# Expert products with weights standing and tokens moving, in blocks of 120 slots

## What is computed

```python
def hier_moe(xn, w_grp, b_grp, w_router, b_router, w_gate, w_up, w_down):
    ...
    eid = grp[:, None].astype(jnp.int32) * EXPERTS_PER_GROUP + top_i.astype(jnp.int32)
    ...
    def expert_block(args):
        xblk, e = args
        hid = jax.nn.silu(xblk @ w_gate[e]) * (xblk @ w_up[e])
        return hid @ w_down[e]
    ...
    return jnp.zeros_like(xn).at[tok_buf].add(yb * w_buf[:, None].astype(yb.dtype))
```

## Time and profile before

| | |
|---|---|
| median of 3 runs | 1314.06 us |
| the profiled execution | 1314.39 us, span 1312.7 us |
| granted TensorE clock, mean over the span | 0.988 |
| PE busy | 1250.6 us (95%) |
| DVE busy | 1049.1 us (80%) |
| ACT busy | 704.0 us (54%) |
| POOL busy | 312.5 us (24%) |

### The profile page before, as it was taken

How to read it: one execution, slowest core, us unless ns; L and a number is a source line. 1 busy time by engine, 2 the same in 40 slices (tenths; PEclk the granted TensorE clock), 3 DMA queues, 4 the chain that set the end, 5 groups by cost and what they waited for, 6 DMA issues and landing times. The chain is left out here.

```text
span 1312.7 us, 23874 instructions
## 1 busy us (share of the span) xinstructions
PE 1250.6 (95%) x8900; PEld 740.3 (56%) x8900; DVE 1049.1 (80%) x1511; ACT 704.0 (54%) x1159; POOL 312.5 (24%) x280
## 2 busy tenths in 40 slices
PE   4999999989999999999999999999998999999995
PEld 2456666656666666666665666654554555555552
DVE  4778777775858999999999686645657999999993
ACT  4556666654234433533342474423311889989983
POOL 1273111110001100110000000001034356667663
PEclk9999999998799999999999999999999999999998
DMA  8700000022214414441442116538578999999982
GB/s 325 176 13 4 0 0 0 15 107 77 41 50 123 107 49 124 106 99 57 120 103 83 50 65 218 181 123 330 208 248 286 311 393 384 392 399 385 368 284 34
DMA packets 53077, 211.27 MB, mean 161 GB/s; under 512 B 14560, under 2 KB 15776, under 8 KB 40416
## 3 DMA queue, kind: packets, MB, share of 16 engines
q1 hardware_dynamic: 31888, 156.95, 32.6%
q0 software_dynamic: 18672, 44.42, 14.3%
q10 hardware_dynamic: 2448, 8.98, 1.7%
HBM read 180.98 MB, written 39.72 MB: 168 GB/s over the span
## 5 line engine op out<-in xcount | busy, mean ns | idle before, releaser
L1329 DVE SCALAR_TENSOR_TENSOR big<-c_region,c_taps,big 128x1024 f32<-128x1024 f32 (+1 forms) x120 | 153.2, 1276 | 3.7 <-ACT caT L1025 3.7
L74 PE MATMUL c_psb<-xnT,w_taken 128*128 128x364 f16 x456 | 145.9, 320 | 0.0
L75 PE MATMUL c_psb<-xnT,w_taken 128*128 128x364 f16 x456 | 145.8, 320 | 0.0
L76 PE MATMUL c_psb<-xnT,f_w_l 128*128 128x364 f16 x456 | 145.7, 320 | 0.0
L1329 DVE SCALAR_TENSOR_TENSOR caT<-c_region,c_taps,caT 128x1024 f32<-128x1024 f32 x112 | 142.9, 1276 | 0.0
L74 PE MATMUL o_psH<-e_gu,big 128*128 128x512 f16 x256 | 97.1, 379 | 2.4 <-issue 1.5
L74 PE MATMUL c_psa<-xnT,w_taken 128*128 128x364 f16 x312 | 99.1, 318 | 0.0
L76 PE MATMUL c_psa<-xnT,f_w_l 128*128 128x364 f16 x312 | 99.0, 317 | 0.0
L75 PE MATMUL c_psa<-xnT,w_taken 128*128 128x364 f16 x312 | 99.0, 317 | 0.0
L76 PE MATMUL o_psH<-e_gu,big 128*128 128x512 f16 x256 | 97.0, 379 | 0.0
L75 PE MATMUL o_psH<-e_gu,big 128*128 128x512 f16 x256 | 97.0, 379 | 0.0
(11 more groups left out here) (397 smaller groups left out, 3455.0 us busy)
## 6 DMA issues: line engine op xcount, KB each, us to landing
e_gu<-w_gu SPq DMA_DIRECT2D x28, 1024.0 KB, 14.0
w_taken<-w_feat SPq DMA_DIRECT2D x48, 512.0 KB, 3.8
e_d<-w_dn SPq DMA_DIRECT2D x15, 1024.0 KB, 17.8
o_room<-w_gu SPq DMA_DIRECT2D x12, 1024.0 KB, 18.6
xnT<-w_gu SPq DMA_DIRECT2D x12, 1024.0 KB, 15.8
big<-w_gu SPq DMA_DIRECT2D x12, 1024.0 KB, 17.4
c_region<-gates POOLq DMA_DIRECT2D x8, 1092.0 KB, 6.0
xnT<-w_dn SPq DMA_DIRECT2D x6, 1024.0 KB, 17.9
```

Source lines behind the costliest of these rows:

```text
L74: pe.matmul(out, stat[0], mov[0], start=start, stop=False)
L75: pe.matmul(out, stat[0], mov[1], start=False, stop=False)
L76: return pe.matmul(out, stat[1], mov[0], start=False, stop=stop)
L1329: dve.scalar_tensor_tensor(y_j, glu[:, p, j:j + SEQ], tap, y_j, op0=ALU.mult, op1=ALU.add).then_inc(tap_done, 1)
```

## The change

The weights become the standing operand of gate and up, 128 columns at a time, and the tokens move. The four column groups j of 128 (two of gate, two of up) each take 8 chunks times 3 matmuls. The result then has the hidden width on partitions, which is the layout that `down` reads, so `turn_hidden` is gone. Gate and up go to separate PSUM banks, and ACT can start on gate before up is done. ACT applies Silu at once in place of the tanh. A block has 120 slots in place of 128. Every expert still has its block, and NOV, the number of places for further blocks, grows from 16 to 18. The arithmetic that finds a token's slot divides by 30 and 120 where it shifted before, by a product and a shift.

```diff
-BLK = 128
-NOV = 16
+BLK = 120
+NOV = 18
 NBLK = NE + 2 * NOV
 NCOL = (T + BLK - 1) // BLK * NE + 1
 RP = 8 + NE
-LANES, LANE_BITS = 4, 5
+LANES = 4
+LANE = BLK // LANES
+PER_LANE, PER_LANE_BITS, LANES_BITS = 2185, 16, 2
...
-        th, sg, hid = (xnT_f[:, rest + 2 * D + i * DE:rest + 2 * D + (i + 1) * DE] for i in range(3))
+        sg, hid = (xnT_f[:, rest + 2 * D + i * DE:rest + 2 * D + (i + 1) * DE].rearrange("p (k n) -> p k n", k=2)[:, :, 0:BLK]
+                   for i in range(2))
...
-        psX = psN[:, 0:2 * P].rearrange("p (k n) -> p k n", k=2)
         psL = psN[:, 2 * P:2 * P + RP]
-        psG = psH[:, 0].rearrange("p (a n) -> p a n", a=2)
-        psY = psH[:, 1]
+        psG = [bank[:, 0:DE].rearrange("p (j n) -> p j n", j=2)[:, :, 0:BLK] for bank in (psH[:, 0, 0:512], psH[:, 0, 512:D])]
+        psU = [bank[:, 0:DE].rearrange("p (j n) -> p j n", j=2)[:, :, 0:BLK] for bank in (psM, psN)]
+        psY = psH[0:BLK, 1]
+        psRows = psT[:, :, 0:BLK]
...
-                pool.indirect_dma_start(out=xg[:, b % 2], out_offset=None, in_=A["hn_dram"],
-                                        in_offset=bass.IndirectOffsetOnAxis(ap=table[:, b:b + 1], axis=0),
+                pool.indirect_dma_start(out=xg[0:BLK, b % 2], out_offset=None, in_=A["hn_dram"],
+                                        in_offset=bass.IndirectOffsetOnAxis(ap=table[0:BLK, b:b + 1], axis=0),
...
-                act.activation(xT_h[:, p], psT[:], ACT.Copy, scale=S_X).then_inc(xT_high, 1)
+                act.activation(xT_h[:, p], psRows, ACT.Copy, scale=S_X).then_inc(xT_high, 1)
 
             def gate(b, p):
-                act.wait_ge(gu_mm, b + 1)
-                act.wait_ge(sg_done, b)
-                act.activation(th, psG[:, p, 0:DE], ACT.Tanh, scale=0.5 * UNSCALE).then_inc(th_done, 1)
+                act.wait_ge(g_mm, b + 1)
+                act.wait_ge(hid_done, b)
+                act.activation(sg, psG[p], ACT.Silu, scale=UNSCALE).then_inc(sg_done, 1)
 
             def hidden(b):
-                act.wait_ge(hT_done, b + 1)
+                act.wait_ge(hid_done, b + 1)
                 act.wait_ge(y_mm, b)
-                act.activation(hT_h, psX, ACT.Copy, scale=0.5 * UNSCALE * UNSCALE * S_H).then_inc(hT_high, 1)
+                act.activation(hT_h, hid, ACT.Copy, scale=UNSCALE * S_H).then_inc(hT_high, 1)
...
             def body(b, p, up, down, u, first=False):
 
                 gate(b, p)
+                act.wait_ge(gu_mm, b + 1)
                 cut(up, p, 0)
...
-                done(dve.tensor_copy(rank_i[:, :, a:b], rank[:, :, a:b]))
-                done(dve.tensor_scalar(level[:, :, a:b], rank_i[:, :, a:b], 7, None, ALU.arith_shift_right))
-                done(dve.tensor_scalar(rank_i[:, :, a:b], rank_i[:, :, a:b], LANE_BITS, None, ALU.arith_shift_right))
+                done(dve.tensor_scalar(rank_i[:, :, a:b], rank[:, :, a:b], float(PER_LANE), None, ALU.mult))
+                done(dve.tensor_scalar(level[:, :, a:b], rank_i[:, :, a:b], PER_LANE_BITS + LANES_BITS, None, ALU.arith_shift_right))
+                done(dve.tensor_scalar(rank_i[:, :, a:b], rank_i[:, :, a:b], PER_LANE_BITS, None, ALU.arith_shift_right))
...
-                dve.scalar_tensor_tensor(xT_l[:, p], psT[:], S_X, xT_h[:, p], op0=ALU.mult,
+                dve.scalar_tensor_tensor(xT_l[:, p], psRows, S_X, xT_h[:, p], op0=ALU.mult,
                                          op1=ALU.subtract).then_inc(xT_low, 1)
 
             def gate(b, p):
 
-                dve.wait_ge(th_done, b + 1)
-                dve.scalar_tensor_tensor(sg, th, 1.0, psG[:, p, 0:DE], op0=ALU.add, op1=ALU.mult).then_inc(sg_done, 1)
                 dve.wait_ge(sg_done, b + 1)
-                dve.wait_ge(hT_done, b)
-                dve.tensor_tensor(hid, sg, psG[:, p, DE:GU], ALU.mult).then_inc(hid_done, 1)
+                dve.wait_ge(gu_mm, b + 1)
+                dve.wait_ge(hT_low, b)
+                dve.tensor_tensor(hid, sg, psU[p], ALU.mult).then_inc(hid_done, 1)
 
             def hidden(b):
                 dve.wait_ge(hT_high, b + 1)
-                dve.scalar_tensor_tensor(hT_l, psX, 0.5 * UNSCALE * UNSCALE * S_H, hT_h, op0=ALU.mult,
+                dve.scalar_tensor_tensor(hT_l, hid, UNSCALE * S_H, hT_h, op0=ALU.mult,
...
-                    last = pe.transpose(psT[:, k, :], xg[:, p, k * P:(k + 1) * P], g.ident[:])
+                    last = pe.transpose(psRows[:, k], xg[0:BLK, p, k * P:(k + 1) * P], g.ident[0:BLK, 0:BLK])
                 last.then_inc(xT_done, 1)
 
-            def gate_up(b, p, first=False, part=range(KC)):
+            def gate_up(b, p, first=False, part=range(4)):
                 if part[0] == 0:
                     pe.wait_ge(gu_low[0], b + 1)
                     pe.wait_ge(gu_low[1], b + 1)
                     pe.wait_ge(xT_low, b + 1)
                     if not first:
                         pe.wait_ge(hid_done, b - 1)
-                for k in part:
-                    last = mm3(pe, psG[:, p], (xT_h[:, p, k, :], xT_l[:, p, k, :]),
-                               (gu_h[:, p, k], gu_l[:, p, k]), k == 0, k == KC - 1)
-                if part[-1] == KC - 1:
-                    last.then_inc(gu_mm, 1)
-
-            def turn_hidden(b):
-                pe.wait_ge(hid_done, b + 1)
-                pe.wait_ge(hT_low, b)
-                for k in range(2):
-                    last = pe.transpose(psX[:, k, :], hid[:, k * P:(k + 1) * P], g.ident[:])
-                last.then_inc(hT_done, 1)
+                for j in part:
+                    cols = slice(j * P, (j + 1) * P)
+                    for k in range(KC):
+                        last = mm3(pe, (psG, psU)[j // 2][p][:, j % 2], (gu_h[:, p, k, cols], gu_l[:, p, k, cols]),
+                                   (xT_h[:, p, k, :], xT_l[:, p, k, :]), k == 0, k == KC - 1)
+                    if j % 2:
+                        last.then_inc((g_mm, gu_mm)[j // 2], 1)
...
-            gate_up(0, 0, True, range(0, HK))
+            gate_up(0, 0, True, range(0, 2))
             turn(1, 1, 0)
-            gate_up(0, 0, True, range(HK, KC))
+            gate_up(0, 0, True, range(2, 4))
             turn(2, 0, 1)
-            turn_hidden(0)
             gate_up(1, 1, True)
             down(0, 0)
             turn(3, 1, 1)
-            turn_hidden(1)
...
                     turn(b + 2, p, 2 * v + i // 2 + 1)
-                    turn_hidden(b)
             b = 4 * few + 6
             gate_up(b, 0)
             down(b - 1, 1)
-            turn_hidden(b)
             gate_up(b + 1, 1)
             down(b, 0, (0,))
-            turn_hidden(b + 1)
             down(b, 0, (1,))
```

More of the change, by code:

```diff
@@ L1815, in ffn_phase @@
         d_high, d_low = sem("e_d_high"), sem("e_d_low")
-        xT_done, xT_high, xT_low, gu_mm, th_done, sg_done, hid_done = (
-            sem("e_" + n) for n in ("xT", "xT_high", "xT_low", "gu_mm", "th", "sg", "hid"))
-        hT_done, hT_high, hT_low, y_mm, y_out = (sem("e_" + n) for n in ("hT", "hT_high", "hT_low", "y_mm", "y_out"))
+        xT_done, xT_high, xT_low, g_mm, gu_mm, sg_done, hid_done = (
+            sem("e_" + n) for n in ("xT", "xT_high", "xT_low", "g_mm", "gu_mm", "sg", "hid"))
+        hT_high, hT_low, y_mm, y_out = (sem("e_" + n) for n in ("hT_high", "hT_low", "y_mm", "y_out"))
         idx_done, idx_y_done = sem("e_idx"), sem("e_idx_y")
@@ L1844, in token @@
         def token(b):
-            return pairs.bitcast(U32)[:, ds(b, 1), 0]
+            return pairs.bitcast(U32)[0:BLK, ds(b, 1), 0]
         def weight(b):
-            return pairs[:, ds(b, 1), 1]
+            return pairs[0:BLK, ds(b, 1), 1]
         def rounds(eng):
@@ L2000, in scatter_static @@
                 pool.indirect_dma_start(out=A["y_all"],
-                                        out_offset=bass.IndirectOffsetOnAxis(ap=table[:, b:b + 1], axis=0),
-                                        in_=y_o[:, b % 2], in_offset=None, compute_op=ALU.add,
+                                        out_offset=bass.IndirectOffsetOnAxis(ap=table[0:BLK, b:b + 1], axis=0),
+                                        in_=y_o[0:BLK, b % 2], in_offset=None, compute_op=ALU.add,
                                         bounds_check=T - 1, oob_is_err=False).then_inc(y_st[b % 2], 16)
@@ L2007, in gather @@
                 pool.wait_ge(xg_ld[p], 16 * u)
-                pool.tensor_copy(idx[:, p:p + 1], token(b)).then_inc(idx_done, 1)
+                pool.tensor_copy(idx[0:BLK, p:p + 1], token(b)).then_inc(idx_done, 1)
                 pool.wait_ge(idx_done, b - 7)
@@ L2017, in scatter @@
                 pool.wait_ge(y_st[p], 16 * u)
-                pool.tensor_copy(idx_y[:, p:p + 1], token(b)).then_inc(idx_y_done, 1)
+                pool.tensor_copy(idx_y[0:BLK, p:p + 1], token(b)).then_inc(idx_y_done, 1)
                 pool.wait_ge(idx_y_done, b - 2)
@@ L2022, in scatter @@
                 pool.indirect_dma_start(out=A["y_all"],
```

(14 more changed lines are left out.)

17 lines of the change are left out of this document (8 added, 9 removed).

## The result

The changed kernel takes 1336.88 us (median of 4 runs, 1334.89 to 1338.79) where the kernel before takes 1314.26 us (1313.55 to 1314.88): ratio 1.0175, interval 1.0162 to 1.0188. It is slower by 22.6 us. I had forecast 1303.0 us.

A forecast was written before the change was run, and what follows sets the result against it. PE and DVE were both taken as full at 8.86 us a block, with DMA behind but hidden by staging. PE's 12.8 us were cut by load landings to 11.3: 1314.39 - 11.3 = 1303.1, stated 1303.0; forecast's own range 1300.5 to 1305.5, 8-in-10 range 1299.5 to 1310.

The forecast's parts named there:

- gate_up: PE, per block: 96 matmuls of 120 columns at 0.0525 us, 5.04 us in place of 5.18, 0.14 us less.
- turn_hidden: PE, per block: the turn of the hidden rows goes, 0.21 us less.
- down: PE, per block: 12 matmuls of 512 columns stay, weight loads of 120 columns lie hidden under them; nothing taken.
- Silu: ACT: Silu replaces the tanh one for one; -0.2 to +0.4 us possible, within ACT's idle time; nothing taken.
- turn: PE, per block: 8 transposes move 120 columns in place of 128; 0 to 0.06 us less, 0.02 taken.
- The 12.8 us of PE: Gain if PE alone decided: 11.8 us from a period of 8.49 us over 32 blocks, 1.0 us at the ends.
- The loads land hardly sooner … because the DMA engines never idle: Weight loads: faster consumers hardly speed landings, so ACT first waits at the cut of 1276.00, whose load lands 7.4 us before.
- how 120 go is not in the trace … 0.1 us a block, 3 us: Gathers: if 15 engines share 120 rows, 6.7% more of 0.56 MB each, ending at 1306 us; within a rival of 17%.
- a wait for loads that starts before block 25: One of the signs listed as showing the forecast wrong; waits of 3 to 5 us were expected only in the last blocks.
- Where the gain meets the transfers: Last blocks: loads limit the gain to 11.7 us, less 0.7 for one more scatter, plus 0.3: 11.3 us.
- The transfers hold more of it back: Rival, 17%: gathers of 120 rows or another slowing of 0.2 us a block end at 1305.5 to 1311 us.
- A further round: Rival, 1%: an expert with more than 120 tokens adds four blocks, 22 us, 1336 us.

The follow-up runs named there:

- e8: The kernel before with only the first half of each down weight loaded from block 7 on: 1313.92 us, ratio 1.0002.
- e7: The kernel of e4 with only the first half of each down weight loaded from block 7 on: 1296.81 us, ratio 0.9871 to the kernel before.
- e4: The changed kernel with only its gathers over 128 rows again, scatters and blocks still 120: 1306.89 us, ratio 0.9947 to the kernel before.
- e3: The changed kernel with blocks of 128 slots and NOV 16, gathers and scatters of 128 rows: 1307.01 us, ratio 0.9948 to the kernel before.
- e1: The changed kernel with gathers and scatters over 128 rows again, blocks still 120 slots: 1307.24 us, ratio 0.9946 to the kernel before.
- e10: The kernel before with each load of down weights as two transfers of 64 partitions, gathers still 128 rows: 1448.71 us, ratio 1.1044.
- e9: The kernel before with the hidden rows' turn set ahead of the next block's turn in the last of the loop's four blocks: 1317.33 us, ratio 1.0033.

## Why the prediction was wrong

*gate_up, turn_hidden, down, Silu* were right: 0.0525 us a matmul, no cost of the weight loads, `down` unmoved, Silu 360 ns. "TensorE: Matmul & The Clock Gate" of the Trainium skill, section "Back-to-back issue gap", has about 81 ns for a matmul of 128 columns with a weight load of its own; this does not hold here, at 52.5 ns for 120 columns and a granted clock of 1.00. *turn* was mis-sized by a little: 0.82 us where I took 0.86. The period came to 8.46 us for the 8.49 forecast.

*The 12.8 us of PE* measured 17.1 (e8 less e7). In their traces the first turn starts at 1006.8 us in both and the last at 1277.0 and 1261.7 us, which is 15.3 us of it: the 28 periods from the fourth turn on, 28 x 0.406 = 11.4 us; the six late fourth blocks, 6 x 0.42 = 2.5 us; and the first three steps, 19.3 us for 17.9 us, 1.4 us. The rest, about 2 us, lies behind the last turn. I had read one period between two turns, 8.86 us, and put it for all 32, so the late blocks were missing.

*"The loads land hardly sooner … because the DMA engines never idle", and "how 120 go is not in the trace … 0.1 us a block, 3 us"* is the step that failed. I priced the gather of 120 rows by its own bytes on 15 engines. What it does is slow the weight loads beside it, which are 84% of all bytes (67.31 of 80.1 MB). A block's 3.71 MB at 339 GB/s are 10.9 us, not 9.5 as at 389: 1.4 us a block, where my rival had 0.1 and, at most, 0.2. The staged weights, of which 7 us were left at the end before, were then used up at 1144 us, around block 16 of 32. Each block after that went at the pace of the loads: the 14 turns after 1147.87 us come 11.1 us apart in the mean. The list of what would prove me wrong did name it, "a wait for loads that starts before block 25", but with no price and hardly a chance.

*Where the gain meets the transfers* had the right mechanism, but what it held back was too small by 4 us, as e4 shows. It also came earlier: ACT first waits for a load at 1210.7 us in e4, some 60 us ahead of the cut at which I had it. I let one more scatter, 0.28 MB, go ahead of the last loads. The queues of e4 from 1030 to 1240 us, to be read against those of the kernel before above:

```profile
q1 hardware_dynamic: 10590, 66.62, 77.1%
q0 software_dynamic: 6967, 13.67, 25.0%
```

The sum is the same, 80.3 and 80.1 MB, but 0.87 MB more of it are gathers and scatters of the blocks that PE has reached sooner, and 0.69 MB less are weights. The load that ACT cuts first at the end, before at 1245.13 + 23.5 = 1268.6, shows it. In e4 it is issued at 1240.53 and takes 31.7 us:

```profile
o_room<-w_gu SPq DMA_DIRECT2D x1, 1024.0 KB, 31.7
```

```profile
1272.27 1.91 ACT L2088 ACTIVATE e_gu<-o_room 128x2048 f16<-128x2048 f32 x1 [0.69 <-DMA o_room<-w_gu]
...
1279.58 1.91 ACT L2094 ACTIVATE e_d<-big 128x2048 f16<-128x2048 f32 x1 [0.80 <-DMA big<-w_dn]
```

It lands at 1272.2, 3.6 us later, and the down load after it 4.0 us later than the 1275.5 of before. 1303.1 and 3.6 to 4.0 us are 1306.7 to 1307.1 us; e4 takes 1306.9. How much of the 3.6 us is the traffic that went ahead, 0.87 MB or 2.2 us, and what the rest is, no run here tells apart.

*The rivals.* "The transfers hold more of it back" looked at the right place, the gather of 120, and had a fourteenth of its price. "A further round" would have given 1336 us, and so near a hit is chance: the number of blocks did not change.

## What to carry to other kernels

Before the row count of a gather goes below 128, or a load is split by partitions, ask what shares the DMA engines with it: here eight rows fewer made the weight loads beside it 15% slower, and carrying eight empty rows undid it. When the DMA engines are busy all the time, their pace is a bound like that of PE, and a period of PE below it only uses up the staged reserve. Read a period over a whole turn of the loop, not between two blocks of it. Two variants with the same time can have different limits (e3 and e4), so look at what each waits for before one part of a change is called worthless.

## What was not expected of the hardware

- A gather into 120, 112 or 104 partitions slows transfers of another queue that run beside it: while it moves, the mean 8 KB packet takes 412 ns for 309 (120 rows). A scatter from 120 partitions costs nothing that can be told (e4 against e1, 1306.89 and 1307.24 us).
- Two loads of 64 partitions each in place of one of 128, same bytes and packet size: 68.9 us of engine time a MB in place of 38.2, though only the down weights, a third of the load, were split.
- The DMA share says nothing of it: it reads 1.02 in the kernel before at 389 GB/s and 1.04 in e10 at 245 GB/s:

```profile
1098.00:1132.00 34.00, 29.43 (x150) 14.80 (x149) 28.02 (x22) 25.25 (x23) 16.39 (x14) 1.00 1.04 245
```

- The branch of this loop costs PE 0.4 us a time when only two short transposes (0.21 us) stand between the last wait and the branch, and nothing with eight (0.87 us, e9).
- A float16 weight load of 120 columns takes 141 ns, one of 128 columns 98 ns. Under matmuls of 0.216 us it does not show.
